# Opening of a two-layer hybrid attention trunk: x squared from its resident tiles, GpSimd for the first low part, a second early gate unit

## The reference, cut to what matters

```python
for i in range(DEPTH):                       # DEPTH 2, x is 512 x 1024
    h = rms_norm(x, attn_norm_w[i])
    proj = h @ w_in[i]
    dq, dk, dv, cq, ckv, krope, xq, gates = jnp.split(proj, IN_SPLIT_POINTS, axis=-1)
    ...                                      # differential attention y_a, latent attention y_b
    mh = rms_norm(mem, mem_norm_w[i])        # mem is 256 x 1024
    mk, mv = jnp.split(mh @ w_mem_kv[i], 2, axis=-1)
    sc = jnp.einsum('bqhd,bkhd->bhqk', xq, mk) * (CROSS_HEAD_DIM ** -0.5)
    pc = jax.nn.softmax(sc, axis=-1)
    co = jnp.einsum('bhqk,bkhd->bqhd', pc, mv)
    y_c = co.reshape(b, s, CROSS_WIDTH) @ w_o_cross[i]
    g_a, g_b, g_c = jnp.split(jax.nn.sigmoid(gates), N_BRANCHES, axis=-1)
    x = x + (g_a * y_a + g_b * y_b + g_c * y_c) @ w_out[i]
    h2 = rms_norm(x, ffn_norm_w[i])
    f_gate, f_up = jnp.split(h2 @ w_gate_up[i], 2, axis=-1)
    x = x + (jax.nn.silu(f_gate) * f_up) @ w_down[i]
return rms_norm(x, final_norm_w)
```

## Time and profile before

| | |
|---|---|
| median of 3 runs | 1957.69 us (1957.12 to 1957.71) |
| the profiled execution, its own time | 1957.46 us |
| its span in the trace | 1955.7 us |
| granted clock, mean | 0.999 |
| PE busy | 1941.7 us, 99% of the span |
| PEld | 1624.6 us, 83% |
| DVE, ACT, POOL busy | 1044.8 us (53%), 929.8 us (48%), 1069.3 us (55%) |
| 128x512 matmuls of the three product lines | 3 x 1568, mean 389 to 395 ns, started 0.23 us apart |
| DMA | 221.02 MB, 113 GB/s over the span |

### The profile page before, as it was taken

How to read it: one execution, slowest core, us unless ns; L and a number is a source line. 1 busy time by engine, 2 the same in 40 slices (tenths; PEclk the granted TensorE clock), 3 DMA queues, 4 the chain that set the end, 5 groups by cost and what they waited for, 6 DMA issues and landing times.

```text
span 1955.7 us, 28646 instructions
## 1 busy us (share of the span) xinstructions
PE 1941.7 (99%) x9252; PEld 1624.6 (83%) x9252; DVE 1044.8 (53%) x1922; ACT 929.8 (48%) x1648; POOL 1069.3 (55%) x1418
## 2 busy tenths in 40 slices
PE   9999999999999999999999999999999999999998
PEld 7888888888888888888888888888888888888887
DVE  5555888887655333321154668888875543333111
ACT  6344666776534222233344456766674442222332
POOL 5655454445555555557765545445445555555674
PEclk9999999999999999999999999999999999999999
DMA  6332333234542322233343333233345322222232
GB/s 249 109 120 92 111 95 102 87 103 142 191 141 87 108 97 97 97 110 97 105 135 121 114 103 104 90 95 105 103 164 181 121 100 94 99 96 93 81 94 90
DMA packets 154035, 221.02 MB, mean 113 GB/s; under 512 B 48338, under 2 KB 65746, under 8 KB 153428
## 3 DMA queue, kind: packets, MB, share of 16 engines
q1 hardware_dynamic: 137040, 184.86, 29.4%
q10 hardware_dynamic: 16900, 34.92, 5.0%
HBM read 198.22 MB, written 21.50 MB: 112 GB/s over the span
## 4 chain that ended last, share of the span: by engine, by line
PE 89%; DVE 8%; ACT 2%; issue 1%; ACTq 0%
PE proj L631 22%; PE proj L633 22%; PE proj L632 22%; PE score L631 2%; PE score L632 2%; PE score L633 2%; PE flip L704 2%; PE score L856 1%; PE score L858 1%; PE score L686 1%; DVE p_b L1857 1%; PE score L870 1%; PE score L690 1%; PE score L689 1%; PE att L612 1%
## 5 line engine op out<-in xcount | busy, mean ns | idle before, releaser
L588 POOL TENSOR_TENSOR w_lo<-raw,w_hi 128x256 fp32r<-128x256 f32 x1372 | 1064.2, 809 | 865.0 <-ACT w_hi L1149 864.7
L631 PE MATMUL proj<-h_hi,w_hi 128*128 128x512 f32 x1568 | 619.0, 395 | 0.0
L633 PE MATMUL proj<-h_hi,w_lo 128*128 128x512 f32 x1568 | 611.3, 390 | 0.0
L632 PE MATMUL proj<-h_lo,w_hi 128*128 128x512 f32 x1568 | 610.5, 389 | 0.0
L1149 ACT ACTIVATE w_hi<-raw 128x1024 fp32r<-128x1024 f32 x344 | 362.5, 1056 | 187.0 <-PE proj L633 55.6
L633 PEld LDWEIGHTS proj<-h_hi,w_lo 128*128 128x128 f32 x1568 | 294.3, 188 | 62.5
L632 PEld LDWEIGHTS proj<-h_lo,w_hi 128*128 128x128 f32 x1568 | 294.7, 188 | 58.1
L631 PEld LDWEIGHTS proj<-h_hi,w_hi 128*128 128x128 f32 x1568 | 294.6, 188 | 58.2 <-issue 0.6
L631 PE MATMUL proj<-hid_hi,w_hi 128*128 128x512 f32 x330 | 129.0, 391 | 0.0
L633 PE MATMUL proj<-hid_hi,w_lo 128*128 128x512 f32 x330 | 128.5, 389 | 0.0
L632 PE MATMUL proj<-hid_lo,w_hi 128*128 128x512 f32 x330 | 128.4, 389 | 0.0
(11 more groups left out here) (409 smaller groups left out, 3142.5 us busy)
## 6 DMA issues: line engine op xcount, KB each, us to landing
raw<-in_w_in SPq DMA_DIRECT2D x224, 256.0 KB, 2.9
raw<-in_w_gate_up SPq DMA_DIRECT2D x176, 256.0 KB, 2.8
raw<-in_w_down SPq DMA_DIRECT2D x96, 192.0 KB, 2.3
gate_in<-gate_scratch ACTq DMA_DIRECT2D x48, 256.0 KB, 4.1
gate_scratch<-gate_out ACTq DMA_DIRECT2D x46, 256.0 KB, 2.0
raw<-in_w_mem_kv SPq DMA_DIRECT2D x32, 256.0 KB, 2.9
raw<-in_w_o_diff SPq DMA_DIRECT2D x32, 256.0 KB, 2.8
raw<-in_w_out SPq DMA_DIRECT2D x32, 256.0 KB, 2.8
```

The costliest lines, as they stand in the source:

```text
L588: ins = g.tensor_tensor(w_lo[s][:, cols], raw[s % 2][:, cols], w_hi[s][:, cols].bitcast(F32), ALU.subtract)
L631: mm(o, hi[:, c:c + width], rh, start=start and k == 0, stop=False)
L632: mm(o, hi[:, c:c + width], rl, start=False, stop=False)
L633: ins = mm(o, lo[:, c:c + width], rh, start=False, stop=stop and k == n - 1)
```

## The change

Nine things change, nearly all before the first 40 us, and a few in stage A of both layers.

1. x is loaded once. The row copy x_row and its four DMAs are gone; tiles 0 and 1 of x have a DMA each, the second one behind slot N0.
2. The sum of squares: ACT squares the eight resident tiles xT (x_squares), DVE adds them in seven 128x512 additions (x_added), PE sums over the partitions with four matmuls onto a column of ones (sum_x, in the middle of unit N2). Root, newton and spread_x as before; spread_x now stands in the middle of unit N3.
3. GpSimd makes the low part of slot N0; DVE no longer does. The four memsets of rope_t on GpSimd come behind the low part of slot N1.
4. In the first unit PE waits for h_hi and h_lo of a tile apart, and takes the w_lo products two by two from tile 4 on.
5. ACT loads the table of Ln and Exp first, starts only two counters at the beginning, and the other 36 behind the copy of slot N1. The sine now needs a table load of its own and comes behind the copy of the slot for project_xq.
6. Stage N has six slots: a second gate unit, N3, in bank flip[0]; the memory units are N4 and N5. Stage A has two gate units. Slots in all are the same number.
7. In layer 0 DVE copies both gate units out of PSUM, and ACT stores them (store_early_gate) at fixed places of its list. In layer 1 ACT copies and stores both.
8. The rope angles on DVE stand behind newton.
9. In stage A split_sum and cross_flip stand between the halves of unit A1; on ACT cross_high stands ahead of the copy of gate unit A1.

```diff
-GATES_N, GATES_A, GATES_Z, GATES_B, GATES_L = 0, 1, 4, 5, 19
+GATES_N, GATES_A, GATES_Z, GATES_B, GATES_L = 0, 2, 4, 5, 19
...
# SyncE
-            load_x(0)
+            sp.dma_start(xT[:, 0, :], x[:, 0, :]).then_inc(in_x_first, 16)
...
                 slot(l, "N", 0, 0, *whole(w_in, l, T_XQ))
                 if l == 0:
+                    sp.dma_start(xT[:, 1, :], x[:, 1, :]).then_inc(in_x_second, 16)
                     for quarter in range(1, 4):
                         load_x(quarter)
                 slot(l, "N", 0, 1, *gate(l, GATES_N))
-                if l == 0:
-                    load_x_row(0)
-                    load_x_row(1)
                 slot(l, "N", 0, 2, *whole(w_in, l, T_CQ))
                 if l == 0:
                     sp.dma_start(memT[:, :, :], mem[:, :, :]).then_inc(in_mem, 16)
-                    load_x_row(2)
-                    load_x_row(3)
-                slot(l, "N", 0, 3, *whole(w_mem_kv, l, 0))
+                slot(l, "N", 0, 3, *gate(l, GATES_N + 1))
...
# GpSimd
-            for s in range(1, 4):
+            for s in range(4):
                 pool.wait_ge(slot_hi.sem, slot_hi.before + s + 1)
+                low(s)
                 if s == 1:
-                    pool.wait_ge(slot_lo.sem, slot_lo.at(0, "N", 0, 1))
-                low(s)
+                    for kind in range(4):
+                        step(g.memset(rope_t[:, kind, :, :], 1.0 - kind % 2))
+                    g.memset(pool_mark[:, 2:3], 0.0).then_inc(const_ready, 1)
...
# TensorE
+            def sum_x():
+
+                pe.wait_ge(const_ready, 4)
+                pe.wait_ge(x_added, KD - 1)
+                for t in range(NT):
+                    ins = mm(att[:, t:t + 1], x_square[:, 0, t * P:(t + 1) * P], ones[:, 0:1], start=True, stop=True)
+                ins.then_inc(x_summed, 1)
...
+                for k in range(KD):
+                    c = slice(k * P, (k + 1) * P)
+                    pe.wait_ge(pair_hi.sem, pair_hi.at(l, "A", 0, k + 1 - KD))
+                    mm(o, w_hi[w][:, c], h_hi[:, k, :], start=k == 0, stop=False)
+                    if k == 4:
+                        pe.wait_ge(slot_lo.sem, slot_lo.at(l, "N", 0, 1))
+                    for q in ((), (), (), (), (0, 1), (2, 3), (4, 5), (6, 7))[k]:
+                        mm(o, w_lo[w][:, q * P:(q + 1) * P], h_hi[:, q, :], start=False, stop=False)
                     pe.wait_ge(pair_lo.sem, pair_lo.at(l, "A", 0, k + 1 - KD))
+                    ins = mm(o, w_hi[w][:, c], h_lo[:, k, :], start=False, stop=k == KD - 1)
...
-                unit(l, "A", 0, 1, 1, None, 4, lambda k: h_rhs(k + 4), first=4 * P, start=False).then_inc(slot_done.sem, 1)
                 split_sum(sum_split.at(l, "A", 0, 1), ssq_read.at(l, "A"), q_sum_hi, q_sum_lo)
                 if l == 0:
                     pe.wait_ge(rope_read, 4)
                 cross_flip(l, i)
-                unit(l, "A", 0, 2, 0, (gate_copied, gate_copied.at(l, "A", 0, 1)), KD, h_rhs).then_inc(slot_done.sem, 1)
+                unit(l, "A", 0, 1, 1, None, 4, lambda k: h_rhs(k + 4), first=4 * P, start=False).then_inc(slot_done.sem, 1)
                 cross_attend(l, i)
...
# ScalarE
-            act.wait_ge(const_ready, 1)
-            start_counts(act, "act")
+            opening = (pair_hi, slot_hi)
+            for t in opening:
+                act.sem_inc(t.sem, 1)
...
-            sc.activation(warm[:, :], warm[:, :], ACT.Sin)
+            sc.preload_act_table_set(LN_EXP)
             act.wait_ge(in_gain, 16)
             first_tile(0)
             first_slot(0)
             for k in range(1, KD):
                 first_tile(k)
             first_slot(1)
+            start_counts(act, "act", opening)
...
+                    x_squares(0, 2)
                     first_slot(2)
+                    x_squares(2, KD)
+                    first_slot(3)
+                    store_early_gate(l, 0)
                     act.wait_ge(in_mem, 16)
                     memory_tiles(l)
+                    root(att[:, 0:NT], x_root, x_summed, 1, x_rooted)
+                    split_ahead(l, "N", 0, 1)
+                    row_squares(mem_row, in_mem_row, mem_ss, mem_squared, 0, NM)
+                    root(mem_ss, mem_root, mem_squared, NM, mem_rooted)
+                    split_ahead(l, "N", 0, 2)
+                    store_early_gate(l, 1)
+                    split_ahead(l, "N", 0, 3)
                     act.wait_ge(pre_vec, 1)
                     sc.activation(sin_t[:, :, :], ang[:, :, :], ACT.Sin)
                     sc.activation(half_t[:, :, :], ang[:, :, :], ACT.Sin, scale=0.5).then_inc(pre_act, 1)
                     sc.preload_act_table_set(LN_EXP)
...
# VectorE
-                if k == 0:
-                    ve.wait_ge(slot_hi.sem, slot_hi.at(0, "N", 0, 1))
-                    ve.wait_ge(slot_lo.sem, slot_lo.at(0, "N"))
-                    v.tensor_tensor(w_lo[0][:, :], raw[0][:, :], w_hi[0][:, :].bitcast(F32), ALU.subtract).then_inc(slot_lo.sem, 1)
+            for n, (a, b) in enumerate(((0, 2), (1, 3), (0, 4), (1, 5), (0, 6), (1, 7), (0, 1))):
+                ve.wait_ge(x_squared, min(n + 3, KD))
+                if n >= 2:
+                    ve.wait_ge(x_added, n - 1 if n < 6 else n)
+                v.tensor_tensor(x_square[:, a, :], x_square[:, a, :], x_square[:, b, :], ALU.add).then_inc(x_added, 1)
...
+                else:
+                    ve.wait_ge(slot_done.sem, slot_done.at(l, "N", 0, 2))
+                    v.tensor_copy(gate_n_raw[:, 0, :], score[1][:, :]).then_inc(gate_copied.sem, 1)
...
+                if l == 0:
+                    ve.wait_ge(x_rooted, 1)
+                    newton(x_root, n=NT, work=x_work, sums=att).then_inc(x_root_ready, 1)
+                    angles()
                 chain(v.memset(q_sum[:, :], 0.0))
...
                 out_xq(l, "N", 0)
                 if l == 0:
+                    ve.wait_ge(slot_done.sem, slot_done.at(l, "N", 0, 4))
+                    v.tensor_copy(gate_n_raw[:, 1, :], flip[0][:, :]).then_inc(gate_copied.sem, 1)
                     ve.wait_ge(mem_sum_full, 1)
```

158 lines of the change are left out of this document (74 added, 84 removed).

## The result

| | before | after |
|---|---|---|
| median, us | 1957.54 (1956.94 to 1958.05, 20 runs) | 1960.16 (1958.76 to 1962.22, 20 runs) |
| ratio to before | | 1.0015, 95% interval 1.0010 to 1.0021 |
| profiled execution, us | 1957.46 | 1961.56 |
| its span, us | 1955.7 | 1959.7 |

The changed kernel is 2.6 us slower, 0.13%, which is under the 0.2% that the prediction calls no change. It forecast +0.6. The single executions also lie further apart than before (3.5 us against 1.1), and the profiled one is 1.4 us above its median, the fifth slowest of the twenty: its trace shows one of the slower cases, and that will matter.

A forecast was written before the change was run, and what follows sets the result against it. PE was taken as the bound, busy 99% of the span, with some 3.8 us to win; -0.4 + 0.25 + 0.7 = +0.55 us on 1957.46 gave a forecast of 1958.1 us, range 1955.6 to 1960.8.

The forecast's parts named there:

- First product at 8.0, not bounded by x: Opening: PE's warm-up ends about when the first product starts (8.01 us), so earlier tiles of x cannot start PE earlier.
- x's tiles stay as they are: Unit N0: h_hi unchanged, seven tiles in 4.66 us, w_hi of N1 at 11.93, as x's last DMA keeps its queue place.
- h_lo slowed, N0 ends at 14.6: Unit N0: GpSimd's pieces slow DVE's h_lo by 0.45 us each; N0 ends at 14.6 against 15.77, gaining 1.15 us.
- Counters 2.5 us: ACT in the opening: 36 counters now come at 11.95 and cost ACT 2.5 us, hidden from PE if N2's w_hi is in time.
- Seven additions: DVE's sum of squares: seven times 0.65 us, four slowed by GpSimd's pieces, 6.35 us, done at 24.0; PE waits 0.3 us.
- sum_x 0.7: Middle of unit N2: sum_x's four matmuls, bounded by none and by the 0.9 us of spread_x's eight, take 0.7 us.
- DVE's chain instead: End of stage N: newton, angles (6.0 us) and gate copy delay the slot's low part; PE starts project_xq at 42.7, not 41.3.
- cross_flip 0.25, stage A 0.7: PE waits 0.25 us at the first cross_flip behind project_xq, and 0.7 us before cross_flip in stage A, for the sin_m copy.
- Table loads of 1.28 without a drain, hidden: ACT behind project_xq: two table loads, 1.28 us each, delay the next slot's low part to 47.3; PE wants it at 48.2.
- Rival 1: DVE's chain 1.4 us or more shorter, PE sets the pace to stage N's end: 1955.6 to 1956.7 us; chance 0.25.
- Rival 4: Opening: x comes later than ACT could take it, N0 still ends at 15.8, hidden: 1958.1 us again; chance 0.08.
- Rival 2: DVE instructions with two SBUF inputs wait whole 0.70 us GpSimd pieces: 1963, milder form 1960.5; chance 0.12, half of it milder.

The follow-up runs named there:

- the filled kernel: Changed kernel with five repairs, eight DVE clearings delaying the last addition, and eight matmuls of unused product ahead of the wait at sum_x: 1959.29 us, ratio 1.0011.

## Why the prediction was right, and where not

"That is no change that can be measured", by the 0.2% that I had set, was right; the size, +0.6 against +2.6, was not. The prediction also named a sign of being wrong, project_xq starting after 45, and in the trace, of one of the slower executions, it starts at 45.65: the account of the opening was wrong though the verdict held. That the verdict held is in part luck, as the wait of 1.4 us that didn't come made up for much of what sum_x lost. By its own steps:

- *First product at 8.0, not bounded by x.* 8.09. But the warm-up is no fixed bound: the traces have the first product anywhere from 7.27 to 8.57 (the last with 0.68 us of waiting for its weights), and it does not decide when N0 ends.
- *x's tiles stay as they are.* Wrong. ACT waited 1.17 and 0.57 us for two transfers of x, and w_hi of N1 came at 12.91 instead of 11.93. I had looked only at the place of the last transfer in the queue.
- *h_lo slowed, N0 ends at 14.6.* 15.34, by another way: h_lo of tile 1 was done at 9.38 instead of 8.5 because x came late, and the six behind it were hardly slowed (9.87 to 13.93), as GpSimd was through by 9.97. Gain 0.43, forecast 1.15. Where x came in time the slowing showed: seven tiles in 7.13 us, 1.02 each, near the 1.1 forecast.
- *Counters 2.5 us.* 1.8 (13.97 to 15.79), but begun 1 us late, so the squares began at 16.16 and the additions at 18.82 instead of 17.6.
- *Seven additions, "of which four meet GpSimd's pieces", done at 24.0, PE waits 0.3.* This is the step that failed. The price, 0.65 + 0.45 = 1.1 us for an addition that meets a piece, was right: 7.55 / 7 = 1.08. The number was wrong: all seven met one, since GpSimd had four clearings of the rope tables ahead (16.82 to 19.10) and then did eight pieces in a row. Begun 1.2 us late and 1.2 longer, they were done at 26.4, and PE waited 1.95.
- *sum_x 0.7.* 0.88, and 0.8 elsewhere. The row to take was there: the trace counts eight matmuls for sum_x, as many as for spread_x (0.9), since both are four in the code.
- *The clock.* Not in the sum at all. I priced a wait at its length. In the profiled execution it fell after the 1.95 us and took another 1.5 us (4.33 us for twelve matmuls, against 2.85 in the filled kernel, 28.31 to 31.16). Whether it falls in the median execution isn't shown: that one is 1.4 us faster than the profiled one, with a wait of 1.1 us there was no fall, and filling the wait did not lower the median (1960.05), so it may well keep its clock. Then the median's +2.6 is that of waits alone, and this is not shown either.
- *No wait at spread_x.* Right.
- *"DVE's chain instead", project_xq at 42.7 and waiting.* Wrong place, right mechanism. Newton's step ended at 31.89 instead of 29.8, the angles took 5.4 us (31.80 to 37.23; forecast 6.0), the gate copy ended at 39.82 instead of 38.3 and the low part at 44.24 instead of 42.6. But PE came at 45.65, and the wait was covered. Where PE was made earlier, with ACT's counters first or the low part on DVE, it showed at once, 0.7 us each.
- *cross_flip 0.25, stage A 0.7.* 0.44 and 0.48. The second went when a tile of A1 was put ahead, and the median fell with the rest.
- *Table loads of 1.28 without a drain, hidden; layer 1 nothing.* Right.
- *Rival 1, PE sets the pace to the end of stage N.* So it was in the trace, but at 45.65 and not at 41.3, because PE itself was held up at sum_x.
- *Rival 4, x later than ACT could take it.* It was, but N0 ended at 15.34 and not 15.8, and the lateness went on to the squares, so it was not hidden.
- *Rival 2, full exclusion.* Its milder form gave 1960.5. The time came out near it, by another way: the exclusion costs 1.08 per addition as forecast, its count and the lateness of x made the rest.

So the sum was: N0 -0.4 for -1.15, sum_x and its wait 2.8 for 1.0, project_xq's wait 0 for 1.4, cross_flip and stage A 0.9 for 0.95, and a clock term of 1.5 in this execution that the sum did not have.

## What to carry to other kernels

When an engine's operations meet another's, count the pieces from the neighbour's own queue in the new order, not from where it worked before: the price per meeting was right to a few hundredths, its number off by three of seven. Give such an addition one operand in PSUM, where a bank is free. Look at what a slower engine off the path holds back: GpSimd's slower low part of N0 kept the raw buffer and so the weights of N2, and this undid most of what ACT had won. And price an idle stretch of PE of two microseconds at more than its length: what fills it, even useless matmuls, can be cheaper than the clock that it loses (1959.29 against 1961.14), though in the changed kernel itself it won nothing (1960.05), and it is better to have the sum in time.

## What the runs showed of the hardware

- The clock fell after idle stretches of 1.95 us (granted 0.85 in the window of 5 us that holds its end, 0.81 in the next) and 2.58 us (0.86, 0.80), and not after 0.48, 0.90 or 1.1 us at the same place. Both times it was still 1.00 while PE stood idle and in the first microsecond of work behind it. Early in N0, just behind the warm-up, less was enough for 0.66 in the window from 10 to 15 us: 1.2 and 0.3 us in one kernel, 0.7 and 0.8 in another (the profiled execution of the kernel with the low part on DVE, 1958.22 where its median is 1956.42); 0.3 and 0.8 us in a third (tile 1 of x apart) were followed by no fall. The falls at sum_x took 1.5 to 1.6 us over twelve matmuls.
- A 128x512 addition with both inputs in SBUF took 1.08 us beside GpSimd's subtractions, which took 1.05 each instead of 0.70; with one input in PSUM it took 0.64, GpSimd working or not. A product of 128x4, both inputs in SBUF, took 0.16 us alone and 0.64 to 0.70 beside those subtractions.
- The 28 warm-up matmuls (14 in the code) took 4.95 to 6.24 us in the traces of the fourteen kernels.
- What makes single executions of the changed kernel 1 to 2 us longer than others stays open. Most kernels with tile 1 of x in a transfer of its own had some at 1961.6 or above, but the last two with it had none above 1959.3, and the two with the sum made late had some without it.
